# One convolution channel group moves from VectorE to ScalarE and GpSimd

## What is computed

```
glu = a * sigmoid(b)                       # 512 channels
c, _ = causal_depthwise(glu, buf, w_dw)    # 31 taps per channel
c = silu(layer_norm(c + b_dw, g, b))
y_conv = c @ w_conv_out
```

## Time and profile before

| | |
|---|---|
| median of three runs | 1665.77 us |
| the profiled execution | 1667.15 us, its span 1665.4 us |
| PE busy | 1535.2 us, 92% |
| DVE busy | 1089.2 us, 65% |
| ACT busy | 811.8 us, 49% |
| POOL busy | 491.4 us, 30% |
| POOL's additions of taps, L555 | 128.9 us, 120 of them |
| taps of layer 0 | between 95 and 281 us |
| taps of layer 1 | between 797 and 982 us |

### The profile page before, as it was taken

How to read it: one execution, slowest core, us unless ns; L and a number is a source line. 1 busy time by engine, 2 the same in 40 slices (tenths; PEclk the granted TensorE clock), 3 DMA queues, 4 the chain that set the end, 5 groups by cost and what they waited for, 6 DMA issues and landing times.

```text
span 1665.4 us, 22890 instructions
## 1 busy us (share of the span) xinstructions
PE 1535.2 (92%) x8707; PEld 1353.6 (81%) x8707; DVE 1089.2 (65%) x1670; ACT 811.8 (49%) x1348; POOL 491.4 (30%) x276
## 2 busy tenths in 40 slices
PE   7999899999799999799998998996999999999995
PEld 6789798887599999778888987974778888888774
DVE  6879795658611011467897956577387877787784
ACT  5645443533333233355454435323466677576673
POOL 0024242000276567300242410011134343343342
PEclk9999898979899999888997989898799999999997
DMA  6322123312355345042222233225377887798780
GB/s 246 124 77 102 52 101 107 127 51 95 114 165 165 119 150 176 1 180 101 98 81 76 77 107 127 72 86 204 111 285 292 328 312 289 263 354 319 271 320 33
DMA packets 57523, 264.66 MB, mean 159 GB/s; under 512 B 9024, under 2 KB 9664, under 8 KB 48448
## 3 DMA queue, kind: packets, MB, share of 16 engines
q1 hardware_dynamic: 57408, 263.11, 44.2%
HBM read 254.54 MB, written 8.54 MB: 158 GB/s over the span
## 4 chain that ended last, share of the span: by engine, by line
PE 39%; DVE 6%; ACT 3%; issue 2%; POOL 1%; POOLq 0%; ACTq 0%; DVEq 0%
PE ps L1340 7%; PE ps L1342 7%; PE ps L1341 7%; PE ps L1288 3%; PE ps L1020 3%; PE ps L1022 2%; PE ps L1021 2%; DVE cacc L1581 1%; DVE Wl L1816 1%; POOL ml L583 1%; ACT mh L901 1%; PE ps L1109 1%; PE ps L1188 1%; PE ps L1227 1%; PE ps L1389 1%
## 5 line engine op out<-in xcount | busy, mean ns | idle before, releaser
L1020 PE MATMUL ps<-Xh,Wl 128*128 128x320 f32 x976 | 336.4, 345 | 25.5 <-DVE Wl L1816 14.2
L1938 DVE TENSOR_TENSOR ml<-mraw,mh 128x1408 fp32r<-128x1408 f32 (+1 forms) x160 | 290.4, 1847 | 76.4 <-ACT mh L901 76.4
L901 ACT ACTIVATE mh<-mraw 128x1408 fp32r<-128x1408 f32 (+1 forms) x216 | 267.9, 1252 | 112.8 <-PE ps L1342 110.3
L1021 PE MATMUL ps<-Xl,Wh 128*128 128x320 f32 x976 | 316.8, 325 | 0.0
L1022 PE MATMUL ps<-Xh,Wh 128*128 128x320 f32 x976 | 316.6, 324 | 0.0
L583 POOL TENSOR_TENSOR ml<-mraw,mh 128x1408 fp32r<-128x1408 f32 (+1 forms) x56 | 178.4, 3185 | 320.5 <-ACT mh L901 320.5
L555 POOL TENSOR_TENSOR cacc<-cacc,G 128x320 f32<-128x320 f32 x120 | 128.9, 1074 | 417.8 <-ACT G L681 408.9
L1020 PEld LDWEIGHTS ps<-Xh,Wl 128*128 128x128 f32 x976 | 197.4, 202 | 49.4 <-issue 29.9
L1816 DVE TENSOR_TENSOR Wl<-raw,Wh 128x1024 fp32r<-128x1024 f32 x138 | 175.6, 1273 | 65.3 <-ACT Wh L610 64.1
L1021 PEld LDWEIGHTS ps<-Xl,Wh 128*128 128x128 f32 x976 | 198.2, 203 | 0.3
L1022 PEld LDWEIGHTS ps<-Xh,Wh 128*128 128x128 f32 x976 | 197.1, 202 | 0.0
(11 more groups left out here) (336 smaller groups left out, 2948.9 us busy)
## 6 DMA issues: line engine op xcount, KB each, us to landing
mraw<-w_moe SPq DMA_DIRECT2D x128, 704.0 KB, 6.5
raw<-w_mix SPq DMA_DIRECT2D x68, 1024.0 KB, 4.7
mraw<-w_moe SPq DMA_DIRECT2D x88, 512.0 KB, 4.7
fraw<-w_ffn SPq DMA_DIRECT2D x44, 512.0 KB, 3.3
fraw<-w_ffn SPq DMA_DIRECT2D x16, 704.0 KB, 3.9
Ss<-st_delta SPq DMA_DIRECT2D x2, 2048.0 KB, 9.0
o_delta_s<-Ss SPq DMA_DIRECT2D x8, 512.0 KB, 2.6
X<-x SPq DMA_DIRECT2D x2, 640.0 KB, 5.5
```

Of the source, the lines that this page charges most:

```text
L901: act.activation(mh[:, n % MS, 0:w], mraw[:, n % MRAW, 0:w], ACT.Copy).then_inc(m_hi, 1)
L1020: pe.matmul(out, wl, xh, start=start, stop=False)
L1021: pe.matmul(out, wh, xl, start=False, stop=False)
L1938: dve.tensor_tensor(ml[:, n % MS, 0:w], mraw[:, n % MRAW, 0:w], mh[:, n % MS, 0:w].bitcast(f32), ALU.subtract).then_inc(m_lod, 1)
```

## The change

One constant. Group 0 stays on DVE; group 1 joins groups 2 and 3 on ACT and POOL. The lists above and the semaphore counts (`conved`, `tap_at`, L332 to L337) are worked out from it, so the places of all taps and of the pooling steps within the chain move.

```diff
--- before
+++ after
@@ -29,7 +29,7 @@
 CHUNK = 64
 WINDOWS = (2, 4, 8, 16)
 GATE_OFF = 3592
-PTAP = 2
+PTAP = 1
 UNIT = 1024
 FUNIT = FT * 128
```

## The result

The changed kernel takes 1652.08 us (median of 4 runs, 1649.16 to 1653.22) against 1666.03 for the kernel before beside it (4 runs, 1664.97 to 1670.49): ratio 0.9914, 95% interval 0.9901 to 0.9926. The forecast was 1650.

The account below looks back on a forecast made before the run. PE was taken as the bound, stalling where DVE answers late. Stalls -8.6 and costs +1.0 gave -7.6 us per layer, -15.2 in all: 1667.15 to 1652 in the profile, 1650.5 in the median, said as 1650; range 1633 to 1672.

Parts of the forecast that it names:

- PE idle in each tap stretch falls from 18 to about 10 us: Sign of the forecast, per layer's stretch with taps; the stretch itself was to fall from 185 to about 177 us.
- The eight priced stalls of layer 1: PE stalls ended by DVE, priced one by one; with +0.7 ahead of t1 they sum to -8.6 us per layer.
- +0.7 ahead of t1: At NT of tile 1, pool(2,1), 1.31 us, now stands ahead of NT's work for a tap of 0.59: +0.7 us.
- DVE's relief, 14 us: DVE's busy time per layer falls by 14 us, 9% of its 155 us, with the added POOL additions counted.
- the middle value: DVE's relief taken as 14 us per layer, between 27.6 us and about 0.
- that has no tap left to hit: Half of the 18.6 us per layer by which POOL's additions hold up DVE's taps, 9.3 us, was to vanish.
- port rival: Every added POOL addition holds up a DVE instruction with two SBUF inputs: 1680 us; chance 0.17 for slower, 0.13 for break-even.
- the break-even: Port case in which each added addition costs 0.61 us of DVE time and the change gives nothing there: 1660 us, chance 0.13.
- ACT late: Rival: ACT's added taps delay Wh, for which DVE waits, 7.2 us per layer cancelling the gain: 1664 us, chance 0.10.
- ACT's stands at the starts of groups: ACT waits at a group's first tap until POOL has added the group before, up to 2.1 us where group 2 begins.
- At break-even only the moved pool parts count: With no gain from the taps, the shifted pooling steps alone would give -(1.9 + 1.5 - 0.7) x 2 = -5.4 us: 1660.
- The clock: PE's half clock after the 2.15 us stall might go with it: 3.5 us more per layer, left out of the sum.

Follow-up runs that it names:

- g_no_add: Changed kernel with POOL's additions for channel group 1 left out and only signalled; ratio 0.9896 to the kernel before, 1647.12 us.
- c_pool_moved: Kernel before, two groups still on DVE, with only the pooling steps shifted to the changed kernel's slots; ratio 1.0032 to the kernel before.
- l_version: Changed kernel with all four groups' taps on ACT and POOL, pool(2) and pool(3) put back, constant matmuls filling two PE stalls; ratio 0.9938, 1653.86 us.
- k_mix: Changed kernel with one pooling step, both parts of pool(2), put back behind t1 of tile 1; ratio 0.9922 to the kernel before.
- f_load: Changed kernel with group 1's taps also made on DVE into an unread buffer, pooling steps in their old slots; ratio 1.0059, 1676.53 us.
- e_relief: Kernel before with 29 of group 1's 31 taps on DVE left out and put nowhere; ratio 0.9868 to the kernel before.
- i_before_busy: Kernel before with constant matmuls on PE ahead of its longest stalls to keep the clock up; ratio 0.9964, 1658.86 us.
- j_after_busy: Changed kernel with constant matmuls on PE ahead of its five longest stalls to keep the clock up; ratio 0.9923 to the kernel before, 1651.65 us.

## Why the prediction came out, and why its steps did not

**The total.** 1650 was forecast; the medians are 1652.08 and 1650.76. The sum behind it was -7.6 us per layer, all of it in the stretches with taps. Measured there, for both layers, is -9.9 in one pair of profiles and -5.6 in the other instead of -15.2. The remainder, 5.8 and 2.5 us, lies outside, where I forecast nothing and where two executions of the unchanged kernel differ by 3 us. The total is right in part by luck.

**The failed step: "PE idle in each tap stretch falls from 18 to about 10 us".** It stayed, at 16.8 and 16.5 us (18.2 and 17.8 in the prediction's terms), and from the first NT of tile 0 to the first gc of tile 2, where the taps end, layer 1 went from 180.7 to 177.9 us, 2.8 less and not 7.6. I had written that I would be wrong if it stayed while DVE's busy time fell, and so the mechanism of the sum is wrong, not only a size: I took each stall as time that PE loses by itself, to be subtracted. The eight priced stalls of layer 1, in the order of the prediction:

| before | forecast | after | measured |
|---|---|---|---|
| 801.12: 1.39 | 0 | 1.36 | 0.0 |
| 834.26: 1.68 | -1.7 | 1.63 | -0.05 |
| 874.78: 2.15 | -1.9 | 0.98 | -1.2 |
| 902.27: 4.67 | -1.8 | 3.14 | -1.5 |
| 937.47: 0.87 | -0.9 | none | -0.9 |
| 948.78: 1.63 | -1.5 | 1.14 | -0.5 |
| 964.93: 0.95 | -0.9 | none | -0.95 |
| 981.82: 2.15 | -0.6 | 1.56 | -0.6 |

Together -5.7 of -9.3 forecast: by themselves these were not badly priced, apart from 834.26, where half of DVE's taps went and nothing changed. In g_no_add, where no additions stand beside this place, the same product starts without a stall:

```profile
823.12 1.10 PE L1191 MATMUL ps<-T,YY 128*128 128x128 f32 x8
```

So it was the added additions that took this relief back. But the text priced only one stall that would grow, +0.7 ahead of t1; that one grew by 2.0 (0.77 to 2.79), the one at T behind it by 1.2 (0.37 to 1.59), and one of 1.41 appeared at gc of tile 1. c_pool_moved and l_version removed named stalls, and others of the same size stood at products nearby, where the shifted pooling steps now lie; k_mix removed one and gained no time.

**"DVE's relief, 14 us".** It is 6.3. 30 additions cost 12.0 us (g_no_add) to 14.4 (f_load), near the 13.6 that the middle value implies. What failed is the 9.3 us of hold-up "that has no tap left to hit". They came in e_relief (0.89 us per tap, against my 0.90), where the taps that stay keep their slots, but not where the list spreads them over the whole stretch: g_no_add, with the 60 old additions alone, has the 18.3 us of the moved taps and none of the 9.3, and 18.3 - 12.0 is the 6.3. In the changed kernel the larger halves of those that stay went from 0.62 to 0.85 us and the smaller ones from 0.43 to 0.71, 15 us over 30 taps: they now stand beside 90 additions and not 60.

**The port rival's mark.** I had set a mean above 0.75 us for 256 columns as the sign of that rival. It is 0.85, and the rival's time, 1660 to 1680, did not come. Its price for the break-even, 0.61 us of DVE time per added addition, was the right one to compare with; the measured 0.40 to 0.48 lie below it. The mean of one line was the wrong mark, since it rises where few taps stand beside many additions, whatever the sum of DVE's time does.

**ACT late.** The waits for Wh rose from 12.2 to 17.3 us, which I had named as its sign. Over the stretch of layer 1, e_relief, without any added work for ACT, waits 24.7, before 15.4 and after 20.4. The sign was wrong and the rival is not shown. ACT's stands at the starts of groups, bounded at 2.1 us, were 1.1 and 0.6.

**The moved pooling steps.** "At break-even only the moved pool parts count", -5.4 us, was a wrong step: alone they cost 0.32% (c_pool_moved).

**The clock.** I left it out and wrote that it might give 3.5 us more per layer, on top of the stalls. It did come up, by 20 and 14 us less at 1.2 GHz in both stretches, half of which is PE's gain in busy time. But i_before_busy and j_after_busy show that it does not come on top: with it held, the gain in the stretches appears as idle time, and the gain in all is 7 us and not 14.

**Why it is faster** is then shown by e_relief and f_load: relief of DVE (-18.7 us in the stretches, -1.32% in all) against the load on POOL and ACT (+13.4 us, +0.59%). What the change gains outside of the stretches, and why moved taps and shifted pooling steps are worth more together than the sum of both, stays open.

## What to carry to other kernels

Where two engines work in turn on one chain, don't subtract stalls one by one: time that leaves one of them can come back at another product, and here the stretches became 19 us shorter with less work on DVE alone, but only 6 with a clock held up for PE, so ask for a run that relieves it alone and one that loads it alone. When work moves from VectorE to GpSimd, price the added GpSimd instructions by what they do to all that stays on VectorE, the remaining part of the same work first, in the places where that part will then stand. A wait of the pacing engine for a helper can be a sign of its spare time and not of the helper's lateness.

## What was not expected of the hardware

A long stall of PE can be followed by a piece at the lower clock: after the stall of 2.15 us the kernel before ran at 0.53 of full clock for 7 us. The stalls of 1.68 us (834.26) and 1.63 us (948.78) in the same layer were not:

```profile
826.00:846.00 20.00, 18.24 (x136) 17.77 (x135) 19.76 (x35) 11.52 (x30) 8.99 (x9) 1.00 0.24 84
940.00:960.00 20.00, 18.00 (x133) 17.53 (x132) 19.50 (x38) 10.64 (x25) 8.24 (x8) 1.00 0.23 70
```

The lower clock after a stall is in the manner of the Trainium skill, TensorE: Matmul & The Clock Gate, section "Part 1: The HAM clock gate", by which the array is throttled unless its activity releases it. Unexpected is how little this costs here: 51 us at 1.2 GHz in the two stretches, of which 25 could have been lost, gave PE 22 us of its own work back, but the stretches only 6 (408.7 to 402.9) and the kernel 0.36% when the clock was held up. And the two layers of one execution differ in the clock and not in idle time: in the changed kernel PE is idle for 16.5 us in each, and one stretch takes 197.96 us, the other 200.68, at a clock of 0.97 and 0.96.
